# Three dilations per head: the order 4, 16, 1 in place of 16, 4, 1

## What is computed

```python
DILATED_CONFIGS = ((128, 1), (512, 4), (2048, 16))     # window, dilation
...
def dilated_mixture(q, k, v, rel_bias):
    outs, lses = [], []
    for window, dil in DILATED_CONFIGS:
        o, lse = dilated_branch(q, k, v, rel_bias, window, dil)
        outs.append(o)
        lses.append(lse)
    w = jax.nn.softmax(jnp.stack(lses, axis=0), axis=0)
    y = jnp.sum(w[..., None] * jnp.stack(outs, axis=0), axis=0)
```

## Time and profile before

| | us |
|---|---|
| median of 3 runs | 1849.25 (1848.52 to 1852.55) |
| the profiled execution | 1847.95 |
| its span | 1846.1 |
| PE busy | 1710.6 (93% of the span) |
| DVE busy | 1179.2 (64%) |
| ACT busy | 806.2 (44%) |

### The profile page before, as it was taken

The page is one execution under the profiler, slowest core; times in us unless marked ns, Lnnn a source line. Parts: engine busy times, 40 slices in busy tenths (PEclk is TensorE's granted clock), DMA queues, the critical chain, the costliest instruction groups (busy, mean ns, idle before and its releaser), DMA issues. The chain is left out here.

```text
span 1846.1 us, 27600 instructions
## 1 busy us (share of the span) xinstructions
PE 1710.6 (93%) x9138; PEld 1459.4 (79%) x9138; DVE 1179.2 (64%) x2323; ACT 806.2 (44%) x1993; POOL 194.5 (11%) x172
## 2 busy tenths in 40 slices
PE   5799999999968999999999999959989899859998
PEld 4577888888856888888888888849989899847886
DVE  5531123333246888888888888836767676665996
ACT  3341122212124555555555555537868687743000
POOL 2102100000000000000000000010222222200231
PEclk9899999999989999999999999977999999979999
DMA  4326855566276548464854453359888888446541
GB/s 165 132 80 227 313 205 182 191 209 211 103 182 183 171 135 256 164 186 145 274 156 156 153 172 132 103 133 211 182 204 182 193 189 190 110 129 225 185 153 60
DMA packets 235236, 320.01 MB, mean 173 GB/s; under 512 B 66781, under 2 KB 160408, under 8 KB 231516
## 3 DMA queue, kind: packets, MB, share of 16 engines
q1 hardware_dynamic: 230620, 308.90, 56.5%
q0 software_dynamic: 2400, 9.48, 1.6%
q10 hardware_dynamic: 2080, 0.01, 0.1%
HBM read 208.38 MB, written 109.94 MB: 172 GB/s over the span
## 5 line engine op out<-in xcount | busy, mean ns | idle before, releaser
L1000 ACT ACTIVATE WT_hi<-wt_ps 128x512 fp32r<-128x512 f32 (+1 forms) x320 | 170.9, 534 | 329.7 <-PE wt_ps L933 329.7
L1046 DVE TENSOR_TENSOR_SCAN W<-w,W,zeros 128x512 f32<-128x512 f32 x192 | 251.3, 1309 | 62.7 <-ACT w L992 61.9
L376 PE MATMUL proj<-h_hi,w_hi 128*128 128x512 f32 x640 | 259.1, 405 | 19.8 <-DVE h_lo L552 17.1
L376 PE MATMUL proj<-h_hi,w_lo 128*128 128x512 f32 x640 | 252.2, 394 | 0.0
L376 PE MATMUL proj<-h_lo,w_hi 128*128 128x512 f32 x640 | 251.8, 393 | 0.0
L1355 ACT ACTIVATE prob<-neg_s,rows 128x256 f32<-128x256 f32 (+1 forms) x384 | 173.5, 453 | 51.7 <-DVE rows L1415 47.8
L1054 DVE TENSOR_TENSOR WT_lo<-wt_ps,WT_hi 128x512 fp32r<-128x512 f32 (+1 forms) x320 | 187.3, 586 | 2.2 <-ACT WT_hi L1000 2.2
L1415 DVE CUSTOM_DVE_ANT_0 neg_s<-s_ps,bias 128x256 f32<-128x256 f32 (+1 forms) x384 | 122.6, 363 | 103.3 <-PE s_ps L1292 92.0
L1291 PE MATMUL s_ps<-k_both,q_hi 128*128 128x256 f32 (+1 forms) x384 | 151.9, 402 | 38.6 <-DMA q_lo<-qk_lo_d 20.6
L933 PE MATMUL wt_ps<-ident,W 128*128 128x128 f32 x1088 | 174.4, 276 | 4.9 <-DVE WT_lo L1054 4.1
L992 ACT ACTIVATE w<-z_ps 128x512 f32<-128x512 f32 (+2 forms) x320 | 169.2, 529 | 20.0 <-PE z_ps L923 20.0
(11 more groups left out here) (134 smaller groups left out, 3363.1 us busy)
## 6 DMA issues: line engine op xcount, KB each, us to landing
wa_hi<-wa_d SPq DMA_DIRECT2D x48, 512.0 KB, 3.8
wa_lo<-wa_d SPq DMA_DIRECT2D x48, 512.0 KB, 4.7
va<-va_d SPq DMA_DIRECT2D x32, 512.0 KB, 11.2
wa_d<-x_sb SPq DMA_DIRECT2D x24, 512.0 KB, 3.9
w_raw<-in_w_tiles SPq DMA_DIRECT2D x18, 512.0 KB, 4.9
moved<-move_d SPq DMA_DIRECT2D x16, 528.0 KB, 4.2
x_sb<-in_x SPq DMA_DIRECT2D x16, 512.0 KB, 5.9
qk_hi_d<-st SPq DMA_DIRECT2D x32, 256.0 KB, 2.9
```

Source lines behind the costliest of these rows:

```text
L376: last = pe.matmul(acc[n % ACC_SLOTS][:], w[w_slot(t)][:, k, :], h[ch][:, k, :], start=(k, a) == (0, 0), stop=(k, a) == (KD - 1, 2))
L1000: act.activation(WT_hi[n % PART_SLOTS][:, cols], t_ps[n % T_SLOTS][:, cols], ACT.Copy) \
L1046: dve.tensor_tensor_scan(W[n % W_SLOTS][:, 0:width][:, ::-1], w[n % W_IN][:, 0:width][:, ::-1], above[:, ::-1], first, ALU.mult, ALU.max). ...
```

## The change

One constant. It sets the order in which a head's bunches stand in the list of steps, and with it the numbers of their banks (`bank_of`), so every wait that counts `rows_done` follows. The orders in which SP loads the values and moves the rows are written out elsewhere and stay as they are: `move` still begins with c = 2.

```diff
     PAIRS = HEADS // TURN_HEADS
     NTILE = TB
-    ORDER = (2, 1, 0)
+    ORDER = (1, 2, 0)
```

## The result

| | us |
|---|---|
| before, median of 4 runs | 1848.88 (1847.41 to 1852.55) |
| order 4, 16, 1, median of 4 runs | 1875.53 (1873.37 to 1881.24) |
| ratio | 1.0146 (95% interval 1.0122 to 1.0171) |
| the profiled execution | 1877.31 |
| its span | 1875.5 |

A forecast was written before the change was run, and what follows sets the result against it. PE's work, taken as the same in any order, bounds the stage. +0.5 start, 0 exchange, -5.8 gates, +5.6 end give +0.3, or +3.4 with three clock falls; taking +1.5, about 1851 us, range 1843 to 1858.

The forecast's parts named there:

- Part 1: In each head, weighing the previous head and starting the next loads come 2.8 us sooner; the head stays at 44 us.
- Part 2: SP's exchange becomes one chain from step 16, 16.0 us, and fits into 17.5 before the weighing.
- I take nothing for all seven: The exchange before the weighing of heads 0 to 6 was claimed to cost 0 us.
- one of the signs of being wrong: The prediction called itself wrong if DVE stands before the weighing (L1448) in heads 0 to 6.
- The exchange is late in every head: Rival: the exchange chain takes 21.6 us against 19.2, costing 17 over seven heads; about 1862 to 1870; chance 0.13.
- Part 3: At three gates DVE's wait shrinks from 7.66 to about 4.9 us, PE's idle time from 5.84 to 4.3; -5.8 in all.
- 0.65 for a fall: Chance given to PE's clock falling at each of the three gates, where 0.9 us is gained with it, 4.0 without.
- Part 4: Ends of the stage: +0.5 us at the start, +5.6 at the last head's weighing.
- the table's forecast: From the stage's start to head 0's weighing: 60.6 us, against 62.9 before.
- +5.6: At the stage's end the last head's weighing comes at 1639.1 instead of 1633.47, since the exchange starts in step 16.
- the middle of +0.3 and +3.4: Sum of all terms with two or with three clock falls at the gates; the prediction gave its middle as +1.5.
- Theory A: From the experiments: a fallen clock stays low through steps of c = 1 and c = 2, with slow strided scores, until c = 0.

The follow-up runs named there:

- experiment 7: Old order, with the store of c = 2 held back until the rows of c = 1 are ready in step 16; 1853.98 us, ratio 1.0025 to the kernel before.
- experiment 8: Old order with four gated output tiles instead of two, so no gating waits for a store; 1842.4 us, ratio 0.9944 to the kernel before.
- experiment 1: The changed kernel with SP's exchange turned, c = 1 moved first and c = 2 behind it; 1863.93 us, ratio 1.0073 to the kernel before.
- experiment 12: New order with the turned exchange and 128 unread extra products in the steps of c = 1 and c = 2; 1847.1 us, ratio 0.9991.
- experiments 4 and 9: Changed kernel with unread extra products: 128 in steps of c = 1 and c = 2, ratio 1.0082; 32 in c = 2 alone, ratio 1.012.
- experiment 3: New order with scores reading neighbouring columns, without strides; 1863.67 us, ratio 1.0075 to the kernel before.

## Why the prediction was wrong

**The step that failed** is the first one: "That work is the same in any order of the bunches, so the change can only matter where something other than PE decides." The number of instructions is the same and their time is not. Of the 30.8 us that the stage lost, 26.7 are PE's busy time, since the mean granted clock went from 0.93 to 0.84. The forecast took the clock for something that only the idle time at the gates can change, and one row of the kernel before spoke against that. I hadn't looked at it: in head 0, before any gate, PE is busy throughout and the clock stays low for 33 us. The row, and PE's first score of c = 0 in that head:

```profile
1239.20:1272.30 33.10, 33.06 (x153) 33.09 (x154) 16.26 (x75) 19.53 (x74) 0.00 (x0) 0.50 1.09 260
```

```profile
1273.25 0.28 PE L1291 MATMUL s_ps<-k_both,q_hi 128*128 128x128 f32 x1
```

The clock is full again at 1272.26, in the last step of c = 1. That row shows what the forecast had ruled out: a low clock with PE busy, whose length goes with the steps that follow. At a gate, in steps of c = 0, a fall is 6.8 us of low clock; behind the weighing of head 0, with five steps of c = 1 and c = 2 still to be scored ahead of c = 0, it is 27.3; at the start of the third turn, with ten, 41.0. But it isn't a rule: at the start of the fourth turn, also with ten, it is 13.7, and in experiments 7 and 8 the clock of the start rises in head 0's sixth step of c = 1. What holds in all five traces with strided scores and without extra work is that the clock never rose in a step that scores c = 2, and that after a fall ahead of c = 0 it was full again by the second step of c = 0.

The Trainium skill ("TensorE: Matmul & The Clock Gate", in "What's actually happening") has it that activity releases the throttle. The rows agree as far as it goes, since with extra products in the steps of c = 2 the clock held there. But being busy was not enough: 40.90 us busy of 40.9 at 0.50.

**Part 1, the weighing sooner: right.** Head 1's bank of step 16 is added at 1327.31 for 0.42, and the weighing starts at 1344.94: 17.2 us between them, where the forecast had 17.5. The loads (L665) start at 1344.76, 17.0 behind that bank, where it was 19.9.

**Part 2, the exchange: right in head 1, wrong in head 0.** The store took 2.75 (forecast 2.7), the time between the reads 9.1 (8.9), and the weighing in head 1 didn't wait. "I take nothing for all seven" missed head 0, where DVE stood before L1448, one of the signs of being wrong that the prediction named. Two things came together there. The start was faster, since the clock rose at 1243.4 instead of 1272.3, and the store stood behind the loads of head 1 and the gate: 7.9 us to be waited for instead of 2.7. DVE stood for 4.66 and PE for 2.52, and at the full price: the clock fell. The rival "The exchange is late in every head" had the mechanism and the wrong reach; it happened in one head of seven. Its price was also summed too low: 1851 and 17 and 5.6 are 1874 and not 1862 to 1870. That this is near the measured time is chance, since the waits it speaks of are not where the time went. In experiment 7, where the start is nearly as slow as before (60.9 us to the weighing of head 0, after 62.9), that weighing doesn't wait.

**Part 3, the gates: right at the first.** There DVE's wait was 4.86 (forecast 4.9). PE's was 4.52 (4.3) and stood before L1317, as forecast, and the clock fell. At the second and third gate DVE waited only 1.85 and 3.34, PE stood for 1.01 and 2.39, and the clock held; both lie behind a stretch at the low clock, which the forecast didn't have. Its 0.65 for a fall can't be judged by this.

**Part 4, the ends.** The start was forecast 0.5 slower and was better by 2.9 than the table's forecast, again by the clock. The end's wait is 5.87, against +5.6. It is the one term of the sum that a run of its own has measured (experiment 7: 5.5). But the last piece lost 14.8 in all, 6.4 more than the 8.4 forecast for it, and in it lies a fall without a pause, 17 us at the low clock. In the sum itself the middle of +0.3 and +3.4 is 1.85 and not 1.5, which changes nothing here.

**The turns' starts were not in the forecast at all.** Before, "issue" held DVE for 3.5 us at most, and PE didn't stand there. Now a turn begins with c = 1, DVE stands for up to 6.87 and PE for 1.41 and 3.33, and the clock falls. That c = 1 covers less is a reading of the timelines. Why DVE takes 6.87 instead of some 3 stays open. With the exchange turned (experiment 1) it is 2.8 at most and there is no fall, but experiment 12, also turned, has 4.3. In the two kernels with extra work and the exchange as the change leaves it (experiments 4 and 9) it is 5.5 to 6.7, with a fall at both turns' starts; in the old order with the late exchange (experiment 7) it is 3.1. So it goes with the new order and the late exchange together. No run was made for this.

**Where the 27 us went,** by the ratios. Turning the exchange takes off 13.5 (1.0146 to 1.0073): the open wait at the end, and the pauses at the turns' starts with the low clock behind them. Thirty-two products in the steps of c = 2 take off 13 more (1.0073 to 1.0004), though they are work of their own: the falls without a pause, and a shorter one behind head 0. What is left can't be told from none. This split holds in this order only: the same products first take off some 5 (1.0146 to 1.012), and the turned exchange behind them 21. Open is why the clock falls at 1516.50 and 1622.31 and not in the same steps of every other head. The three kernels in which it happened without a pause (the changed one, experiments 1 and 8) show only that it was in steps of c = 2, in both orders. Of Theory A, then, what is shown is the cost: PE's clock, low behind pauses ahead of c = 0 and in steps of c = 2. That the strides hold it down is not shown, and that the steps of c = 1 always do is refuted.

## What to carry to other kernels

"PE is busy all the time" doesn't say that PE's time is fixed. Read the granted clock beside the busy share in every stretch, and first in the one where the two disagree. A pause of an engine is priced by what comes behind it: 4.52 us at a gate, among dense steps, cost 6.8 us of low clock, and 1.41 us at a turn's start, ahead of sparse ones, 41. It is a price that varies, since 3.33 us at the next turn's start cost 13.7. So by these runs a wait is better placed in a dense phase (here c = 0) than ahead of a sparse one (c = 1 and c = 2). A small amount of extra work in the sparse phase can pay for itself, and taking one wait away (experiment 8) may bring less than it should until the clock is seen to as well.

When a schedule is reordered, everything that names the old order by hand goes with it. `move` still began with c = 2, and turning it brought back half of the loss.

## What was not expected of the hardware

- The low level can last with PE fully busy: 40.90 of 40.9 us at 0.50 (changed kernel), 37.50 of 37.5 (experiment 8). It can begin so, too, with no pause of PE ahead of it.
- Products that nobody reads made a kernel faster: 32 of them, about 5 us of PE's time, took it from 1.0073 to 1.0004 of the kernel before, 13 us.
- The strided scores don't follow the granted clock. A c = 1 bunch takes 1.08 at 2.4 GHz, and in the changed kernel at 1.2 GHz 1.13 (from 1296.17, the row shown above, to the transposes at 1297.30). Transposes and products beside them take twice as long. Without strides the scores of a c = 2 bunch do follow it: 1.70 at 1.2 GHz (experiment 3) and 0.89 at 2.4. So something other than the array's clock bounds a strided operand, and which part it is no run here shows.
- The same store of 528 KB was landed after 2.75 us with nothing ahead of it and after 7.9 behind the loads of a head and a gate.
